# One layer of a hybrid decoder on one core: the two key blocks of the sliding window joined by a maximum before the turn, the convolution mix in two parts, and the transposes of the next rows spread over VectorE's list

## Chip, core and metric

The kernel runs on one core of a Trainium2 chip, in float32. The time is that of the device, in microseconds, from three runs. Engines: TensorE (PE, with its weight loads PEld), VectorE (DVE), ScalarE (ACT), GpSimd (POOL) and SyncE (SP), which issues most transfers.

## The reference

One layer over 1024 tokens of width 1024. The mixer has two head groups side by side, a gated short convolution (512 channels) and a sliding-window attention (8 query heads, 2 key heads, head size 64, window 128, blocks of 128 queries against the block before and their own); then a mixture of 32 experts, four for each token.

```python
h    = rms_norm(x, norm_mix)
proj = h @ w_in + b_in                      # B_gate | C_gate | u | q | k | v
y_conv = b_gate * causal_short_conv(c_gate * u, conv_w)
# attention: keys are [block before | own block], 256 of them
rel = qi[:, None] + BLOCK - kj[None, :]     # distance of query qi to key slot kj
in_window = (rel >= 0) & (rel < WINDOW)
logits = where(mask, scores + bias, -inf)
m = maximum(max(logits), sink)
p = exp(logits - m)
out = (p / (sum(p) + exp(sink - m))) @ v
mix = concatenate([rms_norm(y_conv), rms_norm(y_attn)])
x = x + mix @ w_out + b_out
x = x + moe_ffn(rms_norm(x, norm_ffn))      # top 4 of 32 experts
```

Window and block are both 128. For a query q and a place s of 0 to 127, key s of the block before is in the window only if s > q, and key s of the own block only if s <= q. Of the two keys at one place exactly one is ever seen (none of the block before in the first block).

## The kernel before

The function mixer handles the 1024 tokens in eight blocks of 128 rows: trip 0 (first=True), a hardware loop over trips 1 to 6, and trip 7 (more=False). The function experts follows it. Each engine has its own list of instructions in program order, written by hand in one_block of that engine; engines meet through semaphores only (wait, then_inc; then_wait makes VectorE wait for its own instruction). An engine whose next instruction waits does nothing behind it.

A trip on TensorE: the convolution's projections for four groups of 128 channels (project_conv, into ps_c), the turn of q and k (L978, L980), the scores (L989, into ps_s: 8 heads x 256 keys), the rest of project_conv, then turn_p (L925: sixteen transposes of 128x128 of the probabilities, eight for each half of four heads, into ps_q, ps_kv and two banks of ps_s), attend (L936, values times pT, into ps_c), the convolution's output mix (L1008, eight matmuls into ps_s, columns 0 to 1023) with the sum of squares of the convolution between its halves (L943), the sum of squares of the attention (L943), the attention's output mix (L1017, into the other half of ps_s), and the projections of q and of k, v for the next block (L885, L889), routing (L904, L1038) among them.

VectorE adds the bias to the scores (add_bias, L694), takes the maximum over 256 keys for each head (L780 and L787), finds the top with the sink (find_top), and adds and divides after the exponentials (normalise: L709, L713, multiply L714 for the first four heads, while ScalarE scales the second four, L574). gate_input (L664) and gate_output (L683) are the convolution's gates; groups 0 and 1 have their taps on VectorE, groups 2 and 3 on GpSimd (add_taps_pool, L456 to L462), which also scales the result into conv_s for the mix (L480 for groups 0 to 2, L484 for group 3). ScalarE takes the exponential (exp_half, L537). The turned probabilities are copied into pT: j=0 by VectorE (read_turned, L730), j=1 by ScalarE (turn_read_act, L544). VectorE turns the normed rows of the next block, xn, into hT by sixteen 32x256 transposes (turn_xn, L622), in parts of 4, 6 and 6; ScalarE scales them (L515), and project_q of the next trip waits for that (hT_ready). VectorE sums conv_sq (L801), makes attnT (L804), sums attn_sq (L809), then updates x1 twice (L824 after the convolution mix, L829 after the attention mix) and makes h2 (L834). GpSimd computes every power of -0.5 (L446) and, in trip 0, copies the bias of the block before over a mask (L474).

## Time and profile before

| | |
|---|---|
| three runs | 1985.57, 1989.87, 1989.88 us (median 1989.87) |
| profiled execution | 1985.67 us, span 1983.9 us |
| TensorE's mean granted clock | 0.988 of full |
| busy: TensorE, VectorE, ScalarE, GpSimd | 1921.2, 1294.7, 430.9, 238.2 us |
| mixer | the first 472 us or so of the span, eight trips |
| TensorE waits in trips 1 to 7 | 2.7 us in six waits of L936 for VectorE's pT, in the window 96 to 430 us |

A row of a timeline names the line of the code, the operation, the tiles out<-in, the size, how many instructions of a kind are merged, and in brackets how long the engine sat idle before it and what ended that. TensorE's instructions overlap: a group's end is modelled, and the start of the next group is the better mark. An f32 matmul shows as two instructions, a transpose as one. A row of busy times by stretch gives the stretch and its length, then busy time (and instructions) of PE, PEld, DVE, ACT and POOL, then the granted clock (1.00 is full), the busy share of the DMA engines, and GB/s.

### The profile page before, as it was taken

How to read it: one execution, taken by the hardware profiler on the slowest of the kernel's cores; microseconds unless marked ns; L12 is line 12 of the kernel's file. 1: busy time of each engine (PE TensorE's matmuls, PEld its weight loads, DVE VectorE, ACT ScalarE, POOL GpSimd, SP SyncE). 2: the span in 40 equal slices, each digit the busy share in tenths (PEclk: the TensorE clock that was granted, in tenths of full speed). 3: DMA queues.
4: the chain of work that ended last, by engine and by line, in shares of the span. 5: the costliest groups of instructions: out<-in, count | busy, mean ns of one | idle time of the engine just before them, and what ended most of it. 6: DMA issues, size and time to landing. Idle time of an engine off the chain costs nothing.

```text
span 1983.9 us, 33393 instructions
## 1 busy us (share of the span) xinstructions
PE 1921.2 (97%) x12288; PEld 1399.4 (71%) x12288; DVE 1294.7 (65%) x3725; ACT 430.9 (22%) x926; POOL 238.2 (12%) x317
## 2 busy tenths in 40 slices
PE   7999999998999999999999999999899999999996
PEld 5667777774999999999999999933334444444442
DVE  2777777774277777776666666644537766777665
ACT  1233333331121222222222222222312100001100
POOL 1212222211000111111111111110000000000000
PEclk8999999998999999999999999999999999999998
DMA  9411001002957787778888898899999999999992
GB/s 311 110 43 42 18 35 42 32 33 86 363 184 237 251 272 250 254 263 288 282 291 297 294 305 298 309 370 383 364 364 384 377 362 354 370 368 369 361 360 72
DMA packets 207682, 498.39 MB, mean 251 GB/s; under 512 B 7716, under 2 KB 14928, under 8 KB 200080
## 3 DMA queue, kind: packets, MB, share of 16 engines
q1 hardware_dynamic: 194016, 449.43, 62.9%
q0 software_dynamic: 11312, 39.85, 8.0%
q10 hardware_dynamic: 2304, 8.39, 1.0%
q8 instruction: 38, 0.62, 0.1%
q14 instruction: 12, 0.10, 0.0%
HBM read 470.24 MB, written 27.41 MB: 251 GB/s over the span
## 4 chain that ended last, share of the span: by engine, by line
issue 36%; PE 36%; POOL 1%; DMA 1%; DVE 1%; POOLq 0%; ACT 0%; DVEq 0%; ACTq 0%
PE ps_unit L1871 36%; POOL x_got L1363 1%; DMA x_got<-h_rows,idx_next 0%; DMA out_dram<-y_rows,idx_cur 0%; PE ps_list L1843 0%; POOL carrier L1359 0%; POOL out_dram L1420 0%; POOLq L1081 0%; POOL out_dram L1375 0%; DVE match L1547 0%; DVE reached L1595 0%; POOLq L1411 0%; POOLq L1250 0%; POOLq L1275 0%; DVE xT L1669 0%
## 5 line engine op out<-in xcount | busy, mean ns | idle before, releaser
L1871 PE MATMUL ps_unit<-xT,w_slot 128*128 128x136 f32 (+6 forms) x3840 | 521.4, 298 | 2.7 <-issue 2.7
L1871 PEld LDWEIGHTS ps_unit<-xT,w_slot 128*128 128x128 f32 x3840 | 516.7, 196 | 2.9 <-issue 2.9
L1901 PE MATMUL ps_unit<-w_slot,xT 128*128 128x512 f32 x704 | 306.7, 594 | 1.1 <-DVE xT L1264 1.1
L1264 DVE STREAM_TRANSPOSE xT<-x_got 32x256 f32<-32x256 f32 x644 | 280.5, 436 | 29.5 <-DMA x_got<-h_rows,idx_next 21.1
L1871 PE MATMUL ps_unit<-act_T,w_slot 128*128 128x136 f32 (+6 forms) x1920 | 261.6, 298 | 0.1
L1871 PEld LDWEIGHTS ps_unit<-act_T,w_slot 128*128 128x128 f32 x1920 | 257.9, 190 | 2.2 <-DVE act_T L1644 1.5
L1901 PEld LDWEIGHTS ps_unit<-w_slot,xT 128*128 128x128 f32 x704 | 132.8, 190 | 164.2 <-issue 164.2
L1660 DVE STREAM_TRANSPOSE y_rows<-yT 32x256 f32<-32x256 f32 x372 | 162.1, 436 | 55.0 <-ACT yT L1466 50.1
L914 PE MATMUL ps_c<-hT,w_in_sb 128*128 128x128 f32 x1536 | 182.5, 279 | 5.4 <-DMA w_in_sb<-in_w_in_dram 5.4
L914 PEld LDWEIGHTS ps_c<-hT,w_in_sb 128*128 128x128 f32 x1536 | 177.7, 194 | 10.7 <-DMA w_in_sb<-in_w_in_dram 6.3
L1359 POOL TENSOR_TENSOR carrier<-carrier 128x1 f32<-128x1 f32 x64 | 15.8, 247 | 1319.8 <-issue 610.6
L1914 PE MATMUL ps_unit<-w_slot,act_T 128*128 128x512 f32 x352 | 154.7, 592 | 0.0
L2031 PE MATMUL ps_unit<-w_slot,xT 128*32 128x512 f32 x1152 | 132.7, 619 | 13.9 <-DVE xT L1264 13.9
L1264 DVE STREAM_TRANSPOSE act_T<-act_rows 32x64 f32<-32x64 f32 x528 | 124.6, 236 | 7.9
L1634 DVE TENSOR_SCALAR glu<-ps_unit,b_cur 128x160 f32<-128x160 f32 (+1 forms) x120 | 50.4, 420 | 109.5 <-PE ps_unit L1871 109.0
L1914 PEld LDWEIGHTS ps_unit<-w_slot,act_T 128*128 128x128 f32 x352 | 66.0, 190 | 78.9 <-issue 78.9
L2031 PEld LDWEIGHTS ps_unit<-w_slot,xT 128*32 128x32 f32 x1152 | 37.9, 113 | 100.5 <-issue 100.3
L1459 ACT ACTIVATE sig<-glu 128x256 f32<-128x256 f32 x120 | 50.0, 417 | 241.9 <-DVE glu L1634 241.7
L1477 ACT ACTIVATE sig<-glu 128x256 f32<-128x256 f32 x44 | 18.3, 416 | 360.4 <-DVE glu L1724 360.4
L1466 ACT ACTIVATE yT<-ps_unit,b_cur 128x256 f32<-128x256 f32 x120 | 50.4, 471 | 208.4 <-PE ps_unit L1871 208.4
L1642 DVE TENSOR_TENSOR sig<-sig,glu 128x160 f32<-128x160 f32 (+1 forms) x120 | 43.7, 364 | 76.9 <-ACT sig L1459 73.5
L1787 DVE TENSOR_TENSOR hid<-ps_unit,b_row 128x512 f32<-128x512 f32 x18 | 12.3, 686 | 90.5 <-PE ps_unit L2031 90.5
(296 smaller groups left out, 1865.0 us busy)
## 6 DMA issues: line engine op xcount, KB each, us to landing
w_slot<-in_w_dram SPq DMA_DIRECT2D x192, 2048.0 KB, 11.1
b_row<-in_b_dram SPq DMA_DIRECT2D x11, 1024.0 KB, 12.9
w_in_sb<-in_w_in_dram SPq DMA_DIRECT2D x6, 1024.0 KB, 12.0
b_row<-in_b_dram SPq DMA_DIRECT2D x11, 512.0 KB, 15.2
x_in<-in_x_dram SPq DMA_DIRECT2D x8, 512.0 KB, 3.5
x_res<-in_x_dram SPq DMA_DIRECT2D x8, 512.0 KB, 4.7
out_dram<-x ACTq DMA_DIRECT2D x8, 512.0 KB, 5.0
h_rows<-h ACTq DMA_DIRECT2D x8, 512.0 KB, 3.1
```

The source lines that it names most:

```text
L914: last = pe.matmul(ps_c[:, c % 2, j * P:(j + 1) * P], w_in_sb[:, k, first:first + P], hT[:, k, :], start=(k == 0), stop=(k == KD - 1))
L1264: last = nc.vector.transpose(out[c * Q:(c + 1) * Q, :, tokens], rows.rearrange("p (k c j) -> p k c j", c=P // Q, j=Q)[:, :, c, :])
L1363: nc.gpsimd.indirect_dma_start(out=x_got[0:n, i, :], out_offset=None, in_=h2_rows, in_offset=bass.IndirectOffsetOnAxis(ap=idx_next[0:n, i: ...
L1459: nc.scalar.activation(sig[:, p % 3, :], glu[:, p % 3, :], ACT.Sigmoid, scale=ALPHA).then_inc(sig_ready[p].sem, 1)
L1466: last = nc.scalar.activation(yT[:, m, :], ps_unit[p % RING][:, u, :], ACT.Identity, bias=b2_cur[:, m:m + 1])
L1634: v.tensor_scalar(glu[:, p % 3, 0:n], ps_unit[p % RING][:, 0, 0:n], b1_cur[:, 2 * p:2 * p + 1], LIMIT, ALU.add, ALU.min).then_inc(glu_read ...
L1642: v.tensor_tensor(sig[:, p % 3, 0:n], sig[:, p % 3, 0:n], glu[:, p % 3, 0:n], ALU.mult).then_inc(scaled[p].sem, 1)
L1660: last = v.transpose(rows[:, :, c, :], yT[c * Q:(c + 1) * Q, :, a * Q:(a + 1) * Q])
L1871: last = pe.matmul(ps_unit[p % RING][:, u, 0:n], w, moving[:, k, 0:n], start=(k == 0), stop=(k == KD - 1))
L1901: last = pe.matmul(ps_hid[c], xT[:, k, 0:P], w_slot[:, c, k, :], start=(k == 0), stop=(k == KD - 1))
L1914: last = pe.matmul(ps_out[m], act_T[:, k, 0:P], w_slot[:, W1_LOADS + m, k, :], start=(k == 0), stop=(k == KD - 1))
L2031: last = pe.matmul(ps_flat[t][g * TILE:(g + 1) * TILE, :], xT[:, k, t * TILE:(t + 1) * TILE], w, start=(k == 0), stop=(k == KD - 1), tile_ ...
```

## The change

Attention: after the bias VectorE joins the two key blocks of each head, place by place, by a maximum into the first 128 columns of probs (join_keys), and reduces these 128 for the top. Exponentials, division and turn then run on 128 columns a head. turn_p has four transposes for each half, into ps_q and one bank of ps_s. VectorE reads each turned half twice, each time multiplied by a 0/1 mask keys_in (own block: tri + identity; block before: one minus that), so that pT has both key blocks again for attend. ScalarE's copies of pT are gone. keys_in is made once, in front of the loop.

TensorE: of the convolution's mix, channel groups 0 and 1 (both output halves) stand before attend, and groups 2 and 3 behind it; the sum of squares of the convolution follows the whole mix. The wait for conv_scaled is in front of the first part, that for conv_scaled_last in front of the second.

VectorE: the transposes of the next rows stand in parts of 2 (before the reads of the turned probabilities), 4, 6 and 4 (behind the mean of the squares, ahead of the first x1 update), where they were in parts of 4, 6 and 6 (the last behind the first x1 update).

```diff
--- before.py
+++ after.py
@@ -218,6 +218,7 @@
         conv_s = sb("conv_s", [P, CC, P])
         probs = sb("probs", [P, NH, 2 * P])
         pT = sb("pT", [P, 2, 2, HALF * P])
+        keys_in = sb("keys_in", [P, 2, P])
         attn_ss = sb("attn_ss", [P, P])
         attnT = sb("attnT", [P, CC, P])
         x1 = sb("x1", [P, D])
@@ -260,7 +261,7 @@
         ps_heads = ps_s[:].rearrange("p (h k) -> p h k", h=NH)
         ps_route = ps_s[:, 1024:1024 + NE]
         ps_parts = ps_s[:, 1536:1536 + P]
-        ps_turned = [[ps_q[:], ps_kv[:]], [ps_s[:, 1024:1536], ps_s[:, 1536:2048]]]
+        ps_turned = [ps_q[:], ps_s[:, 1024:1536]]
 
 
         early_loaded = sem("early_loaded")
@@ -316,7 +317,9 @@
         exped = [event(f"exped_{i}") for i in ("first", "second")]
         denom_ready = event("denom_ready_second")
         probs_ready = [event(f"probs_ready_{i}") for i in ("first", "second")]
-        p_turned = [[event(f"p_turned_{i}{j}") for j in range(2)] for i in ("first", "second")]
+        p_turned = [event(f"p_turned_{i}") for i in ("first", "second")]
+        joined = [event(f"keys_joined_{i}") for i in ("first", "second")]
+        keys_made = sem("keys_made")
         pT_ready = [[event(f"pT_ready_{i}{j}") for j in range(2)] for i in ("first", "second")]
         av_done = event("av_done")
         attn_squared = event("attn_squared")
@@ -534,14 +537,10 @@
                 wait(act, neg_ready[i], t)
                 for h in range(HALF):
                     s = HALF * i + h
-                    nc.scalar.activation(probs[:, s, :], probs[:, s, :], ACT.Exp, bias=neg_top[:, s:s + 1],
+                    nc.scalar.activation(probs[:, s, 0:P], probs[:, s, 0:P], ACT.Exp, bias=neg_top[:, s:s + 1],
                                          accum_out=row_sum[:, s:s + 1])
                 part = slice(i * HALF, (i + 1) * HALF)
                 nc.scalar.activation(sink_exp[:, part], sink_gap[:, part], ACT.Exp).then_inc(exped[i].sem, 1)
-
-            def turn_read_act(t, i):
-                wait(act, p_turned[i][1], t)
-                nc.scalar.copy(pT[:, i, 1, :], ps_turned[i][1]).then_inc(pT_ready[i][1].sem, 1)
 
             square_x(0)
             norm_x(0)
@@ -571,11 +570,9 @@
                 exp_half(t, 1)
                 wait(act, denom_ready, t)
                 for s in range(HALF, NH):
-                    last = nc.scalar.activation(probs[:, s, :], probs[:, s, :], ACT.Copy, scale=rdenom[:, s:s + 1])
+                    last = nc.scalar.activation(probs[:, s, 0:P], probs[:, s, 0:P], ACT.Copy, scale=rdenom[:, s:s + 1])
                 last.then_inc(probs_ready[1].sem, 1)
                 add_u_bias(t, 3)
-                turn_read_act(t, 0)
-                turn_read_act(t, 1)
                 wait(act, conv_out[3], t)
                 nc.scalar.activation(conv_sq[:], conv_y[:], ACT.Square).then_inc(conv_squared.sem, 1)
                 wait(act, attnT_ready, t)
@@ -694,6 +691,15 @@
                 nc.vector.tensor_tensor(probs[:, part, :], ps_heads[:, part, :], bias_all[:, part, :],
                                         ALU.add).then_inc(biased[i].sem, 1)
 
+            def join_keys(t, i):
+
+                part = slice(i * HALF, (i + 1) * HALF)
+                wait(dve, biased[i], t)
+                nc.vector.tensor_tensor(probs[:, part, 0:P], probs[:, part, 0:P], probs[:, part, P:2 * P],
+                                        ALU.max).then_inc(joined[i].sem, 1)
+                wait(dve, joined[i], t)
+                then_wait(t, nc.vector.tensor_reduce(denom[:, part], probs[:, part, 0:P], AX_X, ALU.max))
+
             def find_top(t, i):
 
                 part = slice(i * HALF, (i + 1) * HALF)
@@ -711,8 +717,8 @@
                     nc.vector.reciprocal(rdenom[:, part], denom[:, part]).then_inc(denom_ready.sem, 1)
                     return
                 then_wait(t, nc.vector.reciprocal(rdenom[:, part], denom[:, part]))
-                nc.vector.tensor_tensor(probs[:, part, :], probs[:, part, :],
-                                        rdenom[:, part].unsqueeze(2).broadcast_to([P, HALF, 2 * P]),
+                nc.vector.tensor_tensor(probs[:, part, 0:P], probs[:, part, 0:P],
+                                        rdenom[:, part].unsqueeze(2).broadcast_to([P, HALF, P]),
                                         ALU.mult).then_inc(probs_ready[i].sem, 1)
 
             def turn_h2(t):
@@ -725,9 +731,13 @@
                         last = nc.vector.transpose(h2T[c * 32:(c + 1) * 32, :, a * 32:(a + 1) * 32], rows[:, :, c, :])
                 last.then_inc(h2_squared_off.sem, 1)
 
-            def read_turned(t, i, j):
-                wait(dve, p_turned[i][j], t)
-                nc.vector.tensor_copy(pT[:, i, j, :], ps_turned[i][j]).then_inc(pT_ready[i][j].sem, 1)
+            def read_turned(t, i):
+                wait(dve, p_turned[i], t)
+                for j in range(2):
+                    nc.vector.tensor_tensor(pT[:, i, j, :].rearrange("p (h q) -> p h q", h=HALF),
+                                            ps_turned[i].rearrange("p (h q) -> p h q", h=HALF),
+                                            keys_in[:, j, :].unsqueeze(1).broadcast_to([P, HALF, P]),
+                                            ALU.mult).then_inc(pT_ready[i][j].sem, 1)
 
             dve.wait_ge(cleared, 6)
             x_to_mean(0)
@@ -752,6 +762,10 @@
             nc.vector.tensor_copy(bias_all[:, :, P:2 * P], ps_heads[:, :, P:2 * P]).then_inc(bias_flipped, 1)
             dve.wait_ge(bias_flipped, 2)
             nc.vector.tensor_copy(tri_b[:], cst[:, C_TRI:C_TRI + P])
+            nc.vector.tensor_tensor(keys_in[:, 1, :], cst[:, C_TRI:C_TRI + P], ident, ALU.add).then_inc(keys_made, 1)
+            dve.wait_ge(keys_made, 1)
+            nc.vector.tensor_scalar(keys_in[:, 0, :], keys_in[:, 1, :], -1.0, 1.0, ALU.mult, ALU.add).then_inc(keys_made, 1)
+            dve.wait_ge(keys_made, 2)
             nc.vector.tensor_copy(ones_b[:], cst[:, C_ONES:C_ONES + P])
             nc.vector.scalar_tensor_tensor(out=token[:], in0=cst[:, C_TOK:C_TOK + NB], scalar=32.0,
                                            in1=cst[:, C_TOK + NB:C_TOK + 2 * NB], op0=ALU.mult, op1=ALU.add)
@@ -776,27 +790,27 @@
                 if not first:
                     dve.wait_ge(bias_switched, 1)
                 add_bias(t, 0)
-                wait(dve, biased[0], t)
-                then_wait(t, nc.vector.tensor_reduce(denom[:, 0:HALF], probs[:, 0:HALF, :], AX_X, ALU.max))
+                join_keys(t, 0)
                 wait(dve, scored[1], t)
                 add_bias(t, 1)
                 find_top(t, 0)
                 add_taps(t, 1)
                 gate_output(t, 1)
-                wait(dve, biased[1], t)
-                then_wait(t, nc.vector.tensor_reduce(denom[:, HALF:NH], probs[:, HALF:NH, :], AX_X, ALU.max))
+                join_keys(t, 1)
                 find_top(t, 1)
                 normalise(t, 0)
                 gate_input(t, 2)
                 normalise(t, 1)
                 gate_output(t, 2)
                 gate_input(t, 3)
-                read_turned(t, 0, 0)
-                read_turned(t, 1, 0)
+                if more:
+                    wait(dve, x_normed, t + 1)
+                    turn_xn(t + 1, 0, 2)
+                read_turned(t, 0)
+                read_turned(t, 1)
                 gate_output(t, 3)
                 if more:
-                    wait(dve, x_normed, t + 1)
-                    turn_xn(t + 1, 0, 4)
+                    turn_xn(t + 1, 2, 4)
                 wait(dve, conv_squared, t)
                 nc.vector.tensor_reduce(conv_ss[:], conv_sq[:].rearrange("p c q -> p q c"), AX_X,
                                         ALU.add).then_inc(conv_joined.sem, 1)
@@ -809,11 +823,13 @@
                 nc.vector.tensor_reduce(attn_ss[:], attn_sq.rearrange("p c q -> p q c"), AX_X,
                                         ALU.add).then_inc(attn_joined.sem, 1)
                 if more:
-                    turn_xn(t + 1, 4, 6)
+                    turn_xn(t + 1, 6, 6)
                 wait(dve, attn_summed, t)
                 wait(dve, conv_summed, t)
                 then_wait(t, nc.vector.tensor_copy(ss_ca, ps_kv[:, 2 * P:2 * P + 2]))
                 mean(ss_ca, ms_ca, CW).then_inc(ca_mean.sem, 1)
+                if more:
+                    turn_xn(t + 1, 12, 4)
                 wait(dve, conv_mixed, t)
                 wait(dve, ca_rstd, t)
                 wait(dve, res_biased, t)
@@ -823,8 +839,6 @@
                 dve.wait_ge(late_loaded, all_late)
                 then_wait(t, nc.vector.scalar_tensor_tensor(out=x1[:], in0=ps_s[:, 0:D], scalar=rstd_ca[:, 0:1],
                                                             in1=x_res[:], op0=ALU.mult, op1=ALU.add))
-                if more:
-                    turn_xn(t + 1, 10, 6)
                 wait(dve, attn_mixed, t)
                 nc.vector.scalar_tensor_tensor(out=x1[:], in0=ps_s[:, D:2 * D], scalar=rstd_ca[:, 1:2],
                                                in1=x1[:], op0=ALU.mult, op1=ALU.add).then_inc(x1_ready.sem, 1)
@@ -919,11 +933,17 @@
             def turn_p(t, i):
 
                 wait(pe, probs_ready[i], t)
-                for j in range(2):
-                    for h in range(HALF):
-                        s = HALF * i + h
-                        last = pe.transpose(ps_turned[i][j][:, h * P:(h + 1) * P], probs[:, s, j * P:(j + 1) * P], ident)
-                    last.then_inc(p_turned[i][j].sem, 1)
+                for h in range(HALF):
+                    last = pe.transpose(ps_turned[i][:, h * P:(h + 1) * P], probs[:, HALF * i + h, 0:P], ident)
+                last.then_inc(p_turned[i].sem, 1)
+
+            def mix_conv(ks):
+
+                for n in range(2):
+                    for k in ks:
+                        last = pe.matmul(ps_s[:, n * 512:(n + 1) * 512], conv_s[:, k, :],
+                                         w_out_sb[:, k, n * 512:(n + 1) * 512], start=(k == 0), stop=(k == CC - 1))
+                return last
 
             def attend(t):
 
@@ -997,19 +1017,14 @@
                 project_conv(t, 3)
                 for i in range(2):
                     turn_p(t, i)
-                attend(t)
                 wait(pe, conv_scaled, t)
                 wait(pe, biased[1], t)
                 pe.wait_ge(out_w_loaded, 48)
-                for n in range(2):
-                    for k in range(CC):
-                        if n == 0 and k == CC - 1:
-                            wait(pe, conv_scaled_last, t)
-                        last = pe.matmul(ps_s[:, n * 512:(n + 1) * 512], conv_s[:, k, :],
-                                         w_out_sb[:, k, n * 512:(n + 1) * 512], start=(k == 0), stop=(k == CC - 1))
-                    if n == 0:
-                        sum_squares(t, conv_joined, conv_ss, 0, conv_summed)
-                last.then_inc(conv_mixed.sem, 1)
+                mix_conv((0, 1))
+                attend(t)
+                wait(pe, conv_scaled_last, t)
+                mix_conv((2, 3)).then_inc(conv_mixed.sem, 1)
+                sum_squares(t, conv_joined, conv_ss, 0, conv_summed)
                 sum_squares(t, attn_joined, attn_ss, 1, attn_summed)
                 wait(pe, attnT_ready, t)
                 for n in range(2):
```

## Rows read from the trace of the kernel before

**Rows 1.** The page, busy time of each engine: us (share of the span) xinstructions.
```profile
PE 1921.2 (97%) x12288; PEld 1399.4 (71%) x12288; DVE 1294.7 (65%) x3725; ACT 430.9 (22%) x926; POOL 238.2 (12%) x317
```

**Rows 2.** Busy time by stretch, trip 4: us; PE, PEld, DVE, ACT, POOL; clock, DMA.
```profile
266.00:320.00 54.00, 53.55 (x324) 38.96 (x324) 40.27 (x97) 18.34 (x50) 11.37 (x17) 1.00 0.11 39
```

**Rows 3.** Timeline of TensorE, trips 0 and 4: start us, duration us, what [idle before].
```profile
63.67 1.94 PE L936 MATMUL ps_c<-pT,v_keys 128*64 128x512 f32 x8 [0.46 <-DVE pT L730]
...
80.96 3.24 PE L885 MATMUL ps_q<-w_in_sb,hT 128*128 128x512 f32 x7 [0.67 <-ACT hT L515]
...
279.21 0.60 PE L925 MATMUL ps_q<-cst,probs 128*128 128x128 f32 x4
...
280.08 1.04 PE L925 MATMUL ps_s<-cst,probs 128*128 128x128 f32 x8
...
281.57 1.94 PE L936 MATMUL ps_c<-pT,v_keys 128*64 128x512 f32 x8 [0.45 <-DVE pT L730]
...
283.44 3.70 PE L1008 MATMUL ps_s<-w_out_sb,conv_s 128*128 128x512 f32 x8
...
290.63 0.28 PE L943 MATMUL ps_kv<-cst,attn_ss 128*128 128x1 f32 x2
...
290.77 7.11 PE L1017 MATMUL ps_s<-w_out_sb,attnT 128*128 128x512 f32 x16
...
297.82 7.10 PE L885 MATMUL ps_q<-w_in_sb,hT 128*128 128x512 f32 x16
```

**Rows 4.** Timeline of VectorE, trip 4.
```profile
260.64 0.69 DVE L651 TENSOR_TENSOR qn<-qk,small 128x512 f32<-128x512 f32 x1 [2.08 <-POOL small L446]
...
268.90 1.22 DVE L780 TENSOR_REDUCE small<-probs 128x4 f32<-128x1024 f32 x1
...
274.59 0.16 DVE L709 TENSOR_TENSOR small<-small 128x4 f32<-128x4 f32 x1
...
275.00 1.22 DVE L714 TENSOR_TENSOR probs<-probs,small 128x1024 f32<-128x1024 f32 x1
...
276.14 0.34 DVE L664 SCALAR_TENSOR_TENSOR conv_x<-ps_c,vectors,conv_u 128x128 f32<-128x128 f32 x1
...
276.92 0.41 DVE L709 TENSOR_TENSOR small<-small 128x4 f32<-128x4 f32 x1 [0.44 <-ACT small L540]
...
278.78 0.35 DVE L683 SCALAR_TENSOR_TENSOR conv_y<-ps_c,vectors,conv_t 128x128 f32<-128x128 f32 x1 [1.23 <-POOL conv_t L462]
...
279.88 0.35 DVE L664 SCALAR_TENSOR_TENSOR conv_x<-ps_c,vectors,conv_u 128x128 f32<-128x128 f32 x1 [0.74 <-ACT conv_u L529]
...
280.74 0.68 DVE L730 COPY pT<-ps_s 128x512 f32<-128x512 f32 x1
...
284.58 1.05 DVE L801 TENSOR_REDUCE conv_ss<-conv_sq 128x128 f32<-128x512 f32 x1
...
285.55 0.68 DVE L804 TENSOR_TENSOR attnT<-ps_c,vectors 128x512 f32<-128x512 f32 x1
...
286.89 1.03 DVE L809 TENSOR_REDUCE attn_ss<-qk_sq 128x128 f32<-128x512 f32 x1 [0.66 <-ACT qk_sq L582]
...
293.67 2.70 DVE L622 STREAM_TRANSPOSE hT<-xn 32x256 f32<-32x256 f32 x6
```

**Rows 5.** Timeline of ScalarE, trip 4.
```profile
277.58 1.70 ACT L574 ACTIVATE probs<-probs,small 128x256 f32<-128x256 f32 x4 [0.69 <-DVE small L711]
...
296.40 2.44 ACT L515 ACTIVATE hT<-hT,vectors 128x128 f32<-128x128 f32 x8 [9.54 <-DVE hT L622]
```

**Rows 6.** Timeline of GpSimd, trips 0 and 4.
```profile
63.12 0.83 POOL L480 TENSOR_TENSOR conv_s<-conv_y,vectors 128x384 f32<-128x384 f32 x1
...
276.56 1.11 POOL L456 TENSOR_TENSOR conv_t<-conv_x,vectors 128x128 f32<-128x128 f32 x3 [8.90 <-DVE conv_x L664]
...
279.36 0.83 POOL L480 TENSOR_TENSOR conv_s<-conv_y,vectors 128x384 f32<-128x384 f32 x1 [0.62 <-DVE conv_y L683]
```

**Rows 7.** Busy time by stretch, at the start of the expert stage.
```profile
485.00:490.00 5.00, 4.23 (x21) 2.17 (x22) 3.09 (x17) 0.54 (x2) 2.00 (x2) 0.50 0.27 79
```

## The prediction

> **What bounds the kernel now.** The page comes first: TensorE is busy for 97% of the span [rows 1]. That says little about a single stage, because the change lies in the mixer alone, which is the first 470 us or so. Next comes the table by stretches, cut to one trip of the token block loop. From trip 0 to trip 4 the projection of q moves from 80.96 to 297.82, so a trip takes 54.2 us [rows 3]. Of 54.0 us in trip 4 TensorE is busy 53.5, VectorE 40, ScalarE 18 and GpSimd 11, at a granted clock of 1.00 [rows 2]. So a trip ends when TensorE's own list ends, and the change is worth what it takes off that list, less the waits that it puts in. The timeline of TensorE over the attention's end is read third, for starts rather than busy time, since the ends of matmuls are modelled [rows 3]. The other three engines are read last, each for when it delivers what TensorE will ask for [rows 4 to 6].
>
> **The path that is shortened.** From the first turn of probabilities at 279.21 to the attention's output mix at 290.77 TensorE takes 11.56 us. Its terms are sixteen transposes (279.21 to 280.08 is eight, 0.87, so 1.74 in all, to 280.95), a gap until 281.57 (0.62, ended by the copies of pT; the view shows 0.45 of it as idle), attend (281.57 to 283.44, 1.87), and from there 7.33 for two sums of squares of 0.14 each (290.63 to 290.77) and eight matmuls of the convolution mix, so 3.53 for four of them [rows 3].
>
> **Eight transposes fewer.** They save 0.87 us of that path in each trip. Nothing lies beside them that would keep the time: what they waited for, probs_ready of the second half, is set by ScalarE's four scalings, which end at 279.28 [rows 5]. The turn of the second half would now start at 279.64, and with 128 columns in place of 256 the scalings and exponentials end sooner, not later.
>
> **The gap of 0.62 us.** It is there because attend follows the turn at once and VectorE has to bring the turned blocks over first. In the new order half of the convolution mix (four matmuls, 3.53 us) stands between, and that covers the copies, if it can start. What is late next is conv_s, the input of this half: GpSimd writes it.
>
> **When conv_s comes.** TensorE is through with eight transposes at 279.21 + 0.87 = 280.08. Before, conv_s was done at 279.36 + 0.83 = 280.19, and nobody asked for it before 283.44 [rows 3, 6]. It hangs on a chain: VectorE's gate_input(2) at 276.14, GpSimd's taps from 276.56, gate_output(2) at 278.78, GpSimd at 279.36 [rows 4, 6]. Before gate_input(2) VectorE changes as follows. Each half had a maximum over 128x1024 (268.90, 1.22 us, next start after 1.26). It gets a join over 128x512 and a reduction over 128x512. The trace has no such operations; the nearest are a tensor_tensor of 128x512 from SBUF with 0.69 [rows 4] and, for the reduction, the halved streaming part of the 1.22, about 0.68. With 0.03 for the wait behind each, a half takes 1.43 in place of 1.26: +0.17, twice +0.34. The multiply of the first half's probabilities falls from 1.22 (start to start 1.14) to 0.69 (0.61): -0.53. Net -0.19, so gate_input(2) is at 275.95 and conv_s is done at 280.00. TensorE behind a semaphore started 0.15 after the producer's end (copy 280.74 + 0.68 = 281.42, attend at 281.57), so the mix starts near 280.2: a new wait g of about 0.1 us. There are two more waits in front of this matmul, which may cost a little each; I take g = 0.15. Its bounds: nothing (0.0), if the chain is 0.1 faster; and above, if the reduction costs as much as the strided one of 128x512 (1.05 instead of 0.68, twice [rows 4]), g = 0.15 + 0.74 = 0.9.
>
> **The copies of pT.** ScalarE's two copies go; VectorE has four tensor_tensor with a PSUM source instead of two copies of 0.68 (start to start 0.60, as the multiply's 1.22 gave 1.14). A PSUM source with a broadcast operand is shown by attnT: 0.68 [rows 4]. VectorE: gate_input(3) at 279.88, two transposes 0.89 from 280.14, four reads 2.40 from 281.03 to 283.43, the last result at 283.51. The mix half ends at 280.23 + 3.53 = 283.76, so attend finds all four. Attend runs to 285.63, the second mix half to 289.16, and its last input (conv_s of channel 3) comes from gate_output(3) at 283.43, ended 283.78, plus 0.23 and at most the 0.83 of three groups on GpSimd [rows 6]: 284.8, in time.
>
> **The spread transposes.** Behind gate_output(3) VectorE has four (1.78) to 285.47, the sum over conv_sq (0.97) to 286.44, attnT to 287.12, 0.66 for ScalarE's square to 287.78, the sum over attn_sq (1.03) to 288.81. TensorE asks for it at 289.16 + 0.14 = 289.30. This is 0.35 us of room after latency, where there were 2.7 before (done at 287.92, asked for at 290.63 [rows 3, 4]): the second place to watch. Then six transposes (2.67) to 291.5, the mean (0.3), four more (1.78) to 293.6. hT is complete at 293.6 and no longer at 293.67 + 2.70 = 296.37 [rows 4]. TensorE will want the scaled hT at 289.44 + 7.05 = 296.5 and ScalarE needs half of 2.44 us for its first half [rows 5], so this is free. It must be: before, ScalarE scaled from 296.40, so that hT_ready came at 297.6 and project_q started at 297.82, and a TensorE that is 1.3 us earlier would have run into it. The moved transposes are what lets the gain through.
>
> **Behind the mix.** The second x1 update, h2, its transposes, routing and q/k norms all follow attn_mixed on one chain, which shifts as a whole. The mask keys_in is built once, two VectorE operations of 128 columns in a stretch where VectorE waits for the first convolution weights at the start: nothing, an estimate from their size alone.
>
> **Sum.** A trip: 0.87 + 0.62 - 0.15 = 1.34 us less (bounds 0.6 to 1.5). Trips 1 to 6 and the last one, whose attention is built the same: 7 x 1.34 = 9.4. Trip 0 differs: GpSimd also switches the bias there, so conv_s is done at 63.12 + 0.83 = 63.95 [rows 6], and attend had started at 63.67 [rows 3]. The new order waits until about 63.93 (conv_s 0.19 earlier, plus latency); then 3.53 + 1.87 + 3.53 + 0.28 lead to 73.14 and 7.05 more to 80.19, where project_q had started at 80.96, with 0.67 idle for hT before it. That is 0.8 less. Together 10.2 us. The profiled execution took 1985.67 (span 1983.9), so 1975.5 on its scale. The three timed runs are 1985.57, 1989.87 and 1989.88: the profiled one stands with the lowest, and the median is 4.2 higher. By the median the sum gives 1979.7, by the profile 1975.5; I say **1978**.
>
> **A rule weighed.** An add of 128x4 of two SBUF operands took 0.16 us at 274.59 and 0.41 at 276.92, when GpSimd's taps ran beside it [rows 4, 6]. The Trainium skill, page "SBUF — State Buffer", section on the two separate sides, says that VectorE with two SBUF inputs and a GpSimd instruction that reads SBUF exclude each other for a whole instruction. By that rule, with which the two adds agree, a join could be held or hold the taps. The joins fall at about 268.9 and 273.2, when GpSimd is idle (its taps start at 276.56 [rows 6]), so by rule and row alike the sum stays as it is; were one join per trip held by one tap operation of 0.4 us, the gain would be about 7 us, which is inside rival 1.
>
> **Rivals.** (1) *The wait moves to GpSimd.* The join and reduction cost more than taken, g is 0.5 to 1.0, and a trip gives 0.5 to 1.0 us: seven of them 3.5 to 7, with trip 0's 0.8 some 6 less in all, 1984 by the median. For it: conv_s has no room at all now. Against: every price of 512 columns from SBUF is near 0.7, except the strided reduction. Chance 0.2. (2) *Slower.* The join and the reduction over every second 128 columns run at the price of the 1024-column ones, 1.22 each. Then gate_input(2) is 4 x 0.53 = 2.1 us later, g is 2.25, and a trip loses 2.25 - 1.49 = 0.76: 8 x 0.76 = 6 us more, 1996. It decides from g = 1.49 on. Against it: the ordinary operations are priced by what they stream. Chance 0.05. (3) *The gain is lost behind the mixer.* At the start of the expert stage the clock is granted at half, 0.50 of full from 485 to 490 us [rows 7]; the stage starts earlier against whatever decides on the clock, and the first unit could see the low level for some microseconds more; five at half rate lose 2.5 of work, and as much again if the weights' units behind it slip; I take 5. The three runs, 4.3 apart, show that something of this size is drawn anew. Then 1983 to 1985. Chance 0.13. (4) *The masked read does not fit the room* before the sum over attn_sq: with 0.2 more for each of the four reads, TensorE waits 0.45 a trip, which leaves 0.9 and about 7 us, 1983. Chance 0.07.
>
> **From this the numbers.** Forecast (9 to 12 us less, all mechanisms as told): 0.55. The range is 1971 to 1986: below, the full gain with no new wait on the lower scale (1974) and 3 us of draw; above, rivals 1, 3 and 4. A measurement of this kernel can tell about 0.3%, 6 us, from no change. Faster by more: the forecast, half of the rivals 1 and 4, a third of rival 3: 0.73. Within: the rest of these, 0.21. Slower: rival 2 and a hundredth of rival 3: 0.06.
>
> **What will show it.** TensorE's turn has eight transposes and is followed by mix matmuls within 0.3 us; the stretch to the attention mix is near 10.2 us; a trip is near 52.9 us. Its largest releaser in the loop is GpSimd's conv_s and not VectorE's pT; VectorE's last transpose of hT ends 3 us before project_q. The join and the short reduction are each near 0.69. Wrong if TensorE sits over 0.5 us before the mix or before the sum of squares, if project_q waits for hT, or if the expert stage, from its first weights to its end, is longer than before.

## The result

The changed kernel takes 1975.72 us (median of four runs, 1975.15 to 1976.06); the kernel before, four runs by then, 1988.82 (1985.57 to 1989.88). The ratio is 0.9936, with a 95% interval of 0.9923 to 0.9948: faster by 0.64%. The forecast was 1978, from 1971 to 1986. The profiled execution took 1975.62 us with a span of 1973.8, 10.1 less than before; the sum in the prediction said 10.2. (How much of that agreement is luck is said further down.)

TensorE's timeline of the changed kernel in trip 4, from the turn of the probabilities to the next projection (start, duration, what; compare [rows 3]):

```profile
273.92 0.60 PE L937 MATMUL ps_q<-cst,probs 128*128 128x128 f32 x4
...
274.80 3.70 PE L944 MATMUL ps_s<-w_out_sb,conv_s 128*128 128x512 f32 x8
...
278.43 1.94 PE L956 MATMUL ps_c<-pT,v_keys 128*64 128x512 f32 x8
...
280.30 3.70 PE L944 MATMUL ps_s<-w_out_sb,conv_s 128*128 128x512 f32 x8
...
283.98 0.36 PE L963 MATMUL ps_kv<-cst,attn_ss 128*128 128x1 f32 x2
...
284.20 7.11 PE L1032 MATMUL ps_s<-w_out_sb,attnT 128*128 128x512 f32 x16
...
291.15 7.03 PE L899 MATMUL ps_q<-w_in_sb,hT 128*128 128x512 f32 x16
```

Eight transposes, then at once four matmuls of the mix, with no idle time shown before any of these groups. From the turn (273.92) to the attention mix (284.20) it is 10.28 us, where it was 11.56. From there to project_q it is 6.95, where it was 7.05. The first project_q of the loop, with the wait of trip 0 in front of its mix:

```profile
63.60 3.70 PE L944 MATMUL ps_s<-w_out_sb,conv_s 128*128 128x512 f32 x8 [1.50 <-POOL conv_s L483]
...
79.95 4.46 PE L899 MATMUL ps_q<-w_in_sb,hT 128*128 128x512 f32 x10
```

project_q moves from 79.95 in trip 0 to 291.15 in trip 4, so a trip takes 52.80 us instead of 54.21. VectorE, GpSimd and ScalarE in the same trip (compare [rows 4 to 6]):

```profile
263.61 0.69 DVE L698 TENSOR_TENSOR probs<-probs 128x512 f32<-128x512 f32 x1
...
264.33 0.69 DVE L701 TENSOR_REDUCE small<-probs 128x4 f32<-128x512 f32 x1
...
273.34 0.35 DVE L680 SCALAR_TENSOR_TENSOR conv_y<-ps_c,vectors,conv_t 128x128 f32<-128x128 f32 x1 [1.23 <-POOL conv_t L465]
...
275.74 1.29 DVE L737 TENSOR_TENSOR pT<-ps_q,keys_in 128x512 f32<-128x512 f32 x2
...
276.94 1.28 DVE L737 TENSOR_TENSOR pT<-ps_s,keys_in 128x512 f32<-128x512 f32 x2
...
286.78 1.79 DVE L619 STREAM_TRANSPOSE hT<-xn 32x256 f32<-32x256 f32 x4
```
```profile
273.92 0.83 POOL L483 TENSOR_TENSOR conv_s<-conv_y,vectors 128x384 f32<-128x384 f32 x1 [0.62 <-DVE conv_y L680]
```
```profile
288.61 2.45 ACT L518 ACTIVATE hT<-hT,vectors 128x128 f32<-128x128 f32 x8 [6.03 <-DVE hT L619]
```

conv_s is done at 273.92 + 0.83 = 274.75 and TensorE uses it at 274.80. The masked reads lie at 275.74 to 278.2, beside the first mix part. The last transposes of the next rows end at 288.57, ScalarE's first half of hT 1.2 later, and TensorE asks at 291.15, so hT now has 1.3 us of room.

The mixer ends (first instruction of the expert stage on TensorE) at 461.98, where it was 472.77: 10.8 less. The expert stage takes 1511.8 us from there instead of 1511.1.

### The profile page after: what moved, and what is told of

Read it like the earlier page. It is cut to its first block, busy times and chain, and to the rows that moved or that the text cites. A ratio compares the mean times of both kernels' runs of the same rounds, so it can differ in the third digit from the quotient of the medians.

```text
span 1973.8 us, 33290 instructions
## 1 busy us (share of the span) xinstructions
PE 1912.5 (97%) x12224; PEld 1390.5 (70%) x12224; DVE 1302.9 (66%) x3759; ACT 411.4 (21%) x910; POOL 238.3 (12%) x317
## 4 chain that ended last, share of the span: by engine, by line
PE 39%; issue 35%; POOL 1%; DVE 1%; DMA 0%; POOLq 0%; ACT 0%; DVEq 0%; ACTq 0%
PE ps_unit L1886 38%; POOL x_got L1378 1%; DMA x_got<-h_rows,idx_next 0%; PE ps_list L1858 0%; POOL carrier L1374 0%; POOL out_dram L1435 0%; POOLq L1096 0%; DVE match L1562 0%; POOL out_dram L1390 0%; DVE reached L1610 0%; POOLq L1426 0%; POOLq L1265 0%; DVE xT L1684 0%; ACT xT L1466 0%; POOLq L1413 0%
```

## The experiments

Each was profiled and timed beside the kernel before on the same chip, and the ratios given are to those runs. The changed kernel was not timed again beside them, so its median and theirs come from different sets of runs. Three figures are read for each: the median; the trip, which is the distance of project_q in trips 0 and 6 divided by six; and the mixer's end. The trip is the sharpest. The median also holds the length of the expert stage, which no experiment touches and which lay between 1509.9 and 1516.5 us in the fourteen profiles, with no relation to what had been done in the mixer. The mixer's end also holds what comes ahead of the turn of trip 0, where TensorE waits for the first transfers: that turn started anywhere from 60.21 to 61.98 us (61.30 before, 61.06 in the changed kernel). Where it matters, the end is therefore also counted from that turn.

### Three parts, alone and in pairs

The change has three parts that can stand alone: the join (128 columns, four transposes a half, masked reads), the split mix, and the spread transposes.

**The changed kernel without the spread.** In place of parts of 2, 4, 6, 4:

```diff
-    turn_xn(t + 1, 0, 2)          # ahead of read_turned
-    turn_xn(t + 1, 2, 4)          # behind gate_output(t, 3)
+    turn_xn(t + 1, 0, 4)
-    turn_xn(t + 1, 6, 6)          # behind the sum over attn_sq
+    turn_xn(t + 1, 4, 6)
-    turn_xn(t + 1, 12, 4)         # behind the mean
+    turn_xn(t + 1, 10, 6)         # behind the first x1 update
```

> The changed kernel with the next rows' transposes back in parts of 4, 6 and 6, the last part behind the first x1 update; join and split mix stay. Theory (the gain of TensorE's shorter list passes only because hT is done earlier): VectorE would finish the sum over attn_sq near 282.8 on the clock of the changed kernel's trip 4, six transposes to 285.5, the first x1 update to 288.0 (it waits for GpSimd's root), six transposes to 290.7; ScalarE's first half of the scaling takes 1.2 more, to 292.0, and TensorE asks at 291.15. So project_q waits 0.9 us in each of seven trips: 6 us more than the changed kernel, about 1982, the page names ScalarE's hT as releaser. Rival (hT had room, the new parts are decoration): no wait, 1975.7.

Measured: 1983.9 us, ratio to before 0.9974 (0.9964 to 0.9984), a trip of 54.08. The page of waits names ScalarE's hT six times in six trips, and the timelines of TensorE and VectorE show the chain as it was expected, 0.2 us longer:

```profile
289.00 7.11 PE L1030 MATMUL ps_s<-w_out_sb,attnT 128*128 128x512 f32 x16
...
297.19 7.11 PE L897 MATMUL ps_q<-w_in_sb,hT 128*128 128x512 f32 x16 [1.09 <-ACT hT L518]
```
```profile
291.73 1.28 DVE L836 SCALAR_TENSOR_TENSOR x<-ps_s,small,x_res 128x1024 f32<-128x1024 f32 x1 [1.04 <-POOL small L449]
...
293.05 2.69 DVE L619 STREAM_TRANSPOSE hT<-xn 32x256 f32<-32x256 f32 x6
```

project_q starts 8.19 us after the attention mix and not 6.95. Of the 1.41 us a trip that the whole change brings, 1.28 hang on the moved transposes (54.08 less 52.80). The rival, that hT had room, falls.

**The changed kernel without the split.**

```diff
-    wait(pe, conv_scaled, t)      # and biased, out_w_loaded
-    mix_conv((0, 1))
     attend(t)
-    wait(pe, conv_scaled_last, t)
-    mix_conv((2, 3)).then_inc(conv_mixed.sem, 1)
+    wait(pe, conv_scaled, t)
+    # the eight matmuls as before, sum_squares between the halves
```

> The changed kernel with the convolution mix whole and behind attend, as before; join and spread transposes stay. Theory (the split covers VectorE's four masked reads, which alone hold the second half's first block until 277.6, while the turn ends at 274.8): attend waits 2.8 us a trip and the stretch from turn to attention mix is 12.9 instead of 10.28, trips 1 to 6 lose 2.65 each, the last 1.8 (no transposes of next rows in front of the reads), trip 0 1.0 (conv_s no longer waited for): 19 more, about 1994, slower than the kernel before. Rival (the split only covers the 0.6 us of wait that was there before): 0.5 us a trip, 4 in all, 1980.

Measured: 2000.96 us, ratio 1.0056 (1.0039 to 1.0073). The wait is the expected one, 2.82 us in every trip. But the median is 25 us above that of the changed kernel and not 19, and in the profiled run, the slowest of the four, the mixer ends 28.2 later. The timeline of TensorE shows two kinds of trips; here trips 3 and 4:

```profile
234.42 1.94 PE L956 MATMUL ps_c<-pT,v_keys 128*64 128x512 f32 x8 [2.82 <-DVE pT L737]
...
236.29 3.70 PE L1028 MATMUL ps_s<-w_out_sb,conv_s 128*128 128x512 f32 x8
...
290.00 2.70 PE L956 MATMUL ps_c<-pT,v_keys 128*64 128x512 f32 x8 [2.82 <-DVE pT L737]
...
292.63 4.59 PE L1028 MATMUL ps_s<-w_out_sb,conv_s 128*128 128x512 f32 x8
```

In trip 3 attend takes its usual 1.94 and the mix half 3.70; in trip 4 they take 2.70 and 4.59, behind the same idle 2.82 us. The busy times by stretch of trip 4 have the granted clock in the third number from the end:

```profile
288.00:290.00 2.00, 0.01 (x1) 0.04 (x1) 2.00 (x4) 0.00 (x0) 1.27 (x3) 1.00 0.00 0
...
290.00:292.00 2.00, 2.00 (x8) 0.53 (x8) 1.94 (x5) 0.63 (x1) 1.22 (x2) 0.76 0.00 0
...
292.00:294.00 2.00, 2.00 (x4) 0.84 (x3) 1.97 (x4) 0.00 (x0) 1.49 (x1) 0.50 0.00 0
...
296.00:298.00 2.00, 2.00 (x7) 0.98 (x6) 1.95 (x5) 0.00 (x0) 0.00 (x0) 1.00 0.00 0
```

Behind the gap the granted clock falls to 0.50, the lower of its two levels (1.2 instead of 2.4 GHz), and it is back at 1.00 by 296. project_q follows project_q after 55.57 us in one trip (195.00 to 250.57) and after 57.23 in the next (250.57 to 307.80); this alternates through all trips. So the wait costs 2.77 a trip by itself, and 1.66 more in every second trip through the clock. Why only every second trip, no run shows. The gap of 0.45 in the kernel before, of 1.92 in the next experiment and of 1.35 with the spread alone left the clock at 1.00 in all six trips of the loop. In front of each of these gaps TensorE ran transposes only: from the first of them to attend it is 3.86 us here, 2.96 in the join alone and 3.26 in the spread alone. No run tells which of the two, the idle time or the whole stretch, goes with the fall.

**The join alone** (both edits above together).

> The kernel before with the join alone (128 columns, four transposes a half, masked reads by VectorE); mix whole, transposes of the next rows in parts of 4, 6, 6. Theory (the removed transposes turn into a longer wait for the masked reads): the reads' third result comes near 276.8 with a turn that ends at 274.8, so attend waits 2.0 us where it waited 0.6; a trip loses 0.5 of that net of the 0.87 saved and wins 0.1 at hT: 3 us more than the kernel before in all, about 1988 to 1991. Rival (eight transposes fewer are worth their 0.87 wherever they stand): 7 us less than before, 1979.

```profile
280.20 0.60 PE L935 MATMUL ps_q<-cst,probs 128*128 128x128 f32 x4
...
283.16 1.94 PE L954 MATMUL ps_c<-pT,v_keys 128*64 128x512 f32 x8 [1.92 <-DVE pT L737]
...
285.03 3.70 PE L1026 MATMUL ps_s<-w_out_sb,conv_s 128*128 128x512 f32 x8
...
299.41 7.10 PE L897 MATMUL ps_q<-w_in_sb,hT 128*128 128x512 f32 x16
```

Measured: 1990.23 us, ratio 1.0011 (1.0001 to 1.0022), a trip of 54.81, 0.60 more than before. The turn is 0.87 us shorter and the wait behind it 1.92 long instead of 0.45. The join by itself is a small loss, and the rival of 7 us saved is out by far.

**The split alone** (the split's edit made in the kernel before).

> The kernel before with the mix split in two and nothing else. Theory (hT is the next limit): the 0.6 us of wait for pT goes, but attend ends 3 us later, attnT and the sum over attn_sq with it (to 288.8 instead of 287.9 on the clock of trip 4), and with them the last transposes (to 296.7) and hT's first half (298.0, where TensorE would ask at 297.2 and started at 297.8 before). A trip wins nothing or loses 0.2: 0 to 1.5 more than before. The page names ScalarE's hT as releaser in every trip. Rival (the wait for pT was the loss): 0.5 a trip less, 4 us less than before.

```profile
282.46 3.60 PE L932 MATMUL ps_s<-w_out_sb,conv_s 128*128 128x512 f32 x8
...
291.75 7.11 PE L1020 MATMUL ps_s<-w_out_sb,attnT 128*128 128x512 f32 x16
...
299.95 7.10 PE L885 MATMUL ps_q<-w_in_sb,hT 128*128 128x512 f32 x16 [1.09 <-ACT hT L515]
```

Measured: 1990.86 us, ratio 1.0012 (1.0003 to 1.0022), a trip of 54.84. The direction is the expected one, the size is not: 0.63 a trip and not 0 to 0.2. The stretch to the attention mix is 0.52 shorter, but from there to project_q it is 8.20, 1.15 longer. The expectation had put hT's first half at 298.0 on the clock of the kernel before. The trace, 1.5 later as a whole, has it at 298.53 + 1.25 = 299.8 at the earliest and project_q at 299.95, thus 0.45 later than expected. Two thirds of that lie on VectorE, whose last transposes end at 298.49, which is 297.0 on the old clock where 296.7 had been counted; the rest is the 0.15 from ScalarE's first half to project_q.

**Split and spread without the join.**

> The kernel before with split mix and spread transposes, without the join: sixteen transposes a trip, 256 columns. Theory (the two orders together free the 0.6 us of wait for pT and the hidden 0.1 to 0.2 at hT, the join adds only the eight transposes' 0.87): 0.7 us a trip, 5.5 in all, about 1980 by the profiled scale. Rival (the join is what makes the orders pay): no gain, 1985 to 1988.

Measured: 1983.18 us, ratio 0.9976 (0.9965 to 0.9987), a trip of 53.56 (0.65 less), the mixer's end 466.56 (6.2 less). TensorE has no wait in the loop. Counted from the turn of trip 0, 1.09 us earlier here than before, the mixer is 5.1 shorter, and the medians are 4.2 apart (1987.39 for the kernel before beside it). The profiled run was the slowest of the eight (1984.86), with the longest expert stage of all, 1516.5.

**The spread alone.**

> The kernel before with the next rows' transposes spread and nothing else: the missing corner of the table of three parts. Theory (a spread that puts two transposes ahead of the copies of pT, with no mix half to cover them, lengthens the wait for pT by their 0.89, against 0.17 won at hT): a trip 54.9 instead of 54.2, the mixer's end 4.5 later than before, about 1990, releaser VectorE's pT with 1.3 us. Rival (more room for hT is a gain by itself): 0.17 a trip less, trip 0 0.8, 2 less than before.

```profile
284.84 1.94 PE L938 MATMUL ps_c<-pT,v_keys 128*64 128x512 f32 x8 [1.35 <-DVE pT L730]
...
300.99 7.03 PE L887 MATMUL ps_q<-w_in_sb,hT 128*128 128x512 f32 x16
```

Measured: 1992.02 us, ratio 1.0021 (1.0011 to 1.0031), a trip of 54.99, the mixer's end 4.65 later. This is as expected: project_q comes 6.95 after the attention mix (0.1 won) and attend waits 1.35 instead of 0.45.

The eight corners together:

| join | split | spread | trip, us | mixer's end, us | to before | to before, from trip 0's turn |
|---|---|---|---|---|---|---|
| | | | 54.21 | 472.77 | | |
| x | | | 54.81 | 476.17 | +3.4 | +4.1 |
| | x | | 54.84 | 475.65 | +2.9 | +3.7 |
| | | x | 54.99 | 477.42 | +4.7 | +4.4 |
| x | x | | 54.08 | 470.60 | -2.2 | -1.8 |
| x | | x | 56.40 | 490.20 | +17.4 | +18.2 |
| | x | x | 53.56 | 466.56 | -6.2 | -5.1 |
| x | x | x | 52.80 | 461.98 | -10.8 | -10.6 |

Each part alone makes the mixer slower. The three together make it faster by more than any pair does.

### The terms, one by one

**Eight transposes put back** in the changed kernel:

```diff
     last.then_inc(p_turned[i].sem, 1)
+    spare = [ps_kv[:], ps_s[:, 1536:2048]][i]
+    for h in range(HALF):
+        pe.transpose(spare[:, h * P:(h + 1) * P], probs[:, HALF * i + h, P:2 * P], ident)
```

> The changed kernel with the eight dropped transposes put back, of the unused second 128 columns into free banks that nobody reads: the price of eight transposes by itself. Theory: 0.87 a trip less what conv_s was late by (0.1 at most), so 0.8; in trip 0 the wait for conv_s of 1.5 hides them: 7 x 0.8 = 5.6 more, 1981.3. Rival (the transposes lie beside a wait that would be there anyway): less than 2 us more.

```profile
275.94 0.60 PE L937 MATMUL ps_q<-cst,probs 128*128 128x128 f32 x4
...
277.68 3.60 PE L947 MATMUL ps_s<-w_out_sb,conv_s 128*128 128x512 f32 x8
...
281.21 1.94 PE L959 MATMUL ps_c<-pT,v_keys 128*64 128x512 f32 x8
```

Measured: 1982.9 us (0.9981, 0.9971 to 0.9991), a trip of 53.56, 0.76 more than the changed kernel. The turn takes 0.87 more (275.94 to 277.68 is 1.74), and the first mix part 0.10 less (3.53 instead of 3.63), because conv_s is then there long before. That is 0.77. The mixer's end moves by 5.0, or 5.3 from trip 0's turn. A trip of 53.56 is also what split and spread have without the join: all that the join wins is these transposes, and its other halvings (exponentials, maxima, scalings) win nothing on TensorE's list.

**conv_s later by one GpSimd instruction:**

```diff
     wait(pool, conv_mixed, t - 1)
+    nc.gpsimd.tensor_tensor(scratch[:], conv_y[:, 0:3, :], conv_g_col...)   # 128x384, then wait
     nc.gpsimd.tensor_tensor(conv_s[:, 0:3, :], ...)
```

> The changed kernel with one more GpSimd instruction of 128x384 (0.83 us, result unused) in front of the one that makes conv_s: the wait for conv_s lengthened by a known piece. Theory (conv_s has no room: it is ready as the turn ends): the whole of 0.87 shows in each of eight trips, 7 us more, 1982.7, releaser GpSimd's conv_s. Rival (conv_s comes well ahead and its closeness in the trace is chance): under 2 us more.

```profile
277.51 0.60 PE L942 MATMUL ps_s<-cst,probs 128*128 128x128 f32 x4
...
278.87 3.70 PE L949 MATMUL ps_s<-w_out_sb,conv_s 128*128 128x512 f32 x8 [0.75 <-POOL conv_s L488]
```

Measured: 1981.64 us (0.9968, 0.9956 to 0.9979), a trip of 53.70, so the whole delay shows (0.90 a trip, for 0.87 put in). The mixer's end is 6.8 later, or 7.2 from trip 0's turn. conv_s has no room.

**The sum over attn_sq done twice:**

```diff
     wait(dve, attn_squared, t)
+    nc.vector.tensor_reduce(scratch[:], attn_sq..., AX_X, ALU.add)          # then wait
     nc.vector.tensor_reduce(attn_ss[:], attn_sq..., AX_X, ALU.add)
```

> The changed kernel with the sum over attn_sq done twice (first into a scratch tile), 1.07 us more on VectorE in front of attn_joined. Theory (the room there is 0.3 us in trips 1 to 6, 1.2 in trip 0, and several us in the last): TensorE waits 0.75 in six trips, 4.5 us more, 1980.2; hT still has room and takes nothing. Rival (VectorE's delay also reaches hT or the x1 chain): a whole 1.07 or more in each of seven trips, 7.5 us more.

```profile
287.61 0.38 PE L968 MATMUL ps_kv<-cst,attn_ss 128*128 128x1 f32 x2 [0.63 <-DVE attn_ss L828]
...
294.81 5.74 PE L904 MATMUL ps_q<-w_in_sb,hT 128*128 128x512 f32 x13
```

Measured: 1979.29 us (0.9953, 0.9936 to 0.9969), a trip of 53.61, 0.81 longer for 1.07 put in. So the room there was 0.26, and 0.3 had been counted. hT, which VectorE delivers behind it, did not get a wait (project_q again 6.95 behind the attention mix).

### Further edits to the changed kernel

**The switch of the bias in trip 0 behind conv_s** (GpSimd's L477 of the changed kernel moved two lines down).

> The changed kernel with GpSimd's switch of the bias in trip 0 behind conv_s of groups 0 to 2 instead of in front. Theory: trip 0's wait of 1.5 us for conv_s goes, and what is next there (the sum over attn_sq, ready at 71.6, asked for at 71.4) leaves 1.4: 1974.3. Rival (the microseconds of trip 0 are given back at the start of the expert stage, whose first transfers come when they come): 1975.7.

```profile
60.24 0.60 PE L937 MATMUL ps_q<-cst,probs 128*128 128x128 f32 x4
...
71.11 0.38 PE L963 MATMUL ps_kv<-cst,attn_ss 128*128 128x1 f32 x2 [0.49 <-DVE attn_ss L823]
...
78.30 1.88 PE L899 MATMUL ps_q<-w_in_sb,hT 128*128 128x512 f32 x4
```

Measured: 1973.76 us (0.9937, 0.9923 to 0.9951). From the turn to project_q trip 0 takes 18.06 us instead of 18.89: 0.83 won and not 1.4, because the sum over attn_sq is asked for earlier and now has a wait of 0.49 there. The timed runs are too coarse for it: the ratio to the kernel before is that of the changed kernel (0.9936), and the 2 us between the medians are from two sets of runs. In the profile the turn of trip 0 also starts earlier (60.24 for 61.06), within what it varies by without any edit.

**conv_s in two parts that match the two parts of the mix:**

```diff
+    for i in range(2):
+        wait(pool, conv_out[i], t)
+    wait(pool, conv_mixed, t - 1)
+    nc.gpsimd.tensor_tensor(conv_s[:, 0:2, :], ...).then_inc(conv_scaled.sem, 1)
     add_taps_pool(t, 2)
     ...
-    nc.gpsimd.tensor_tensor(conv_s[:, 0:3, :], ...).then_inc(conv_scaled.sem, 1)
     add_taps_pool(t, 3)
-    nc.gpsimd.tensor_tensor(conv_s[:, 3:4, :], ...).then_inc(conv_scaled_last.sem, 1)
+    nc.gpsimd.tensor_tensor(conv_s[:, 2:4, :], ...).then_inc(conv_scaled_last.sem, 1)
```

> The changed kernel with conv_s made in two parts that match the two parts of the mix: groups 0 and 1 in front of the taps of group 2 (their inputs are there 3 us earlier), groups 2 and 3 at the end. Theory: conv_s is off the path in every trip; trip 0 wins 1.4, the others the 0.09 by which the first mix half was longer than the second: 2.0 less, 1973.7. Against it: GpSimd's new instruction reads beside VectorE's join of the second half, and if one holds the other by 0.6 us, group 2's gate comes later; that has over 1 us of room now, since nothing of group 2 is asked for before the second mix half.

Measured: 1971.96 us in five runs (1971.12 to 1972.77), ratio to before 0.9926 (0.9912 to 0.994); the changed kernel's four runs lie at 1975.15 to 1976.06, but its ratio, 0.9936 (0.9923 to 0.9948), is not clear of this one. What shows the gain is the trace. A trip is 52.68, 0.12 less, and trip 0 takes 17.13 from the turn to project_q, 1.76 less. Together 2.6, where 2.0 was expected, and 2.6 is also what the mixer's end gains from trip 0's turn. The first mix part takes 3.53 again in every trip. GpSimd's two instructions of one shape, the first beside VectorE's join (266.02 to 266.70), the second not:

```profile
266.24 0.93 POOL L475 TENSOR_TENSOR conv_s<-conv_y,vectors 128x256 f32<-128x256 f32 x1 [5.76 <-issue]
...
276.69 0.61 POOL L488 TENSOR_TENSOR conv_s<-conv_y,vectors 128x256 f32<-128x256 f32 x1 [1.30 <-DVE conv_y L681]
```
```profile
266.02 0.68 DVE L699 TENSOR_TENSOR probs<-probs 128x512 f32<-128x512 f32 x1
```

The same 128x256 takes 0.93 and 0.61, and so it is in all eight trips (0.93 or 0.94 against 0.61). 0.93 less 0.61 is 0.32, and the join ends 0.46 after GpSimd's start. The Trainium skill, page "SBUF — State Buffer", section on the two separate sides, says that of a VectorE instruction with two SBUF inputs and a GpSimd instruction that reads SBUF the one that starts first holds the other off until it is through. The rows agree in kind: the join started first, and GpSimd was the slower for it. In size they don't quite: 0.61 from the join's end on would have ended 0.14 later than it did. No row shows why.

**The sum of squares of the convolution between the output halves,** on top of that (the sum behind the first of them and not behind both).

> As the kernel with early scaling, and the convolution's sum of squares between the two output halves of the second mix part instead of behind them, so that the two sums are not back to back (0.22 us for the second, where it was 0.14 alone). Theory: 0.08 a trip, 0.6 more saved, 1973.1. Rival: the 0.22 is a wait for attn_joined, and then nothing is saved.

```profile
278.98 1.98 PE L1029 MATMUL ps_s<-w_out_sb,conv_s 128*128 128x512 f32 x4
...
280.80 0.28 PE L964 MATMUL ps_kv<-cst,conv_ss 128*128 128x1 f32 x2
...
282.74 0.28 PE L964 MATMUL ps_kv<-cst,attn_ss 128*128 128x1 f32 x2
...
282.88 7.11 PE L1038 MATMUL ps_s<-w_out_sb,attnT 128*128 128x512 f32 x16
```

Measured: 1972.1 us (six runs, 1968.54 to 1974.55; 0.9924, 0.991 to 0.9938), a trip of 52.68, the same as without it. The second sum is back at 0.14, but from 278.98 to 282.88 it is 3.90, and it was 3.90 before (278.31 to 282.21). So the 0.22 was no wait for attn_joined. Moving the first sum between the halves wins nothing: what the second sum has less, the mix around the first has more. What the 0.08 is the price of stays open.

## Why the prediction was right

**The list of TensorE.** The prediction took 0.87 us off for the transposes, 0.62 for the gap, and put 0.15 in for conv_s: 1.34 a trip. Measured in the stretch: 1.28. The transposes are confirmed by putting them back (0.87 in the turn), the gap by its absence. The new wait is no wait in the view: conv_s comes at 274.75 and the matmul starts 0.05 later, not 0.15 (0.05 also in trip 0 and with conv_s delayed, where TensorE does wait), and what is left is a first mix part that is 0.10 longer (3.63 for 3.53; 3.53 again once conv_s comes early). What the prediction did not have is 0.08 more for the two sums, which stand side by side now; parting them did not win it back.

**hT.** The prediction let project_q start 7.05 behind the attention mix, as before, and its figures left hT 0.2 us of room there (ready at 297.6, used at 297.82). It had none: in every kernel with the spread project_q starts after 6.95, and the split alone lost 1.15 there. The mechanism ("a TensorE that is 1.3 us earlier would have run into it") is what the kernel without the spread shows. It is the step on which most of the gain hung: without it 8.6 of the 10.8 us of the mixer are gone. The 0.10 won at hT, and 0.04 ahead of the turn, stood in no term. They more than make up for the 0.06 by which the stretch fell short, and a trip came to 1.41 less, not 1.34.

**conv_s.** Predicted done at 280.00, with the turn ending at 280.08, on the clock of the kernel before; that is 0.08 ahead of the end. The trace has 274.75 against 273.92 + 0.87 = 274.79: 0.04 ahead. The prices of the unseen operations held: join 0.69, reduction 0.69 (0.68 taken), multiply 0.69. Rival 1 (the wait moves to GpSimd) has its place right, as the delay of 0.87 that came out whole shows, and not its size (0.10 a trip for its 0.5 to 1.0); rival 2 (slower, at the price of 1024 columns) falls with the 0.69.

**The second place.** Room before the sum over attn_sq: 0.35 predicted, 0.26 by the experiment. The reads cost 0.60 from start to start, as taken, so rival 4 falls.

**Trip 0.** Predicted: conv_s waited for until 63.93, project_q 0.8 earlier. Measured: a mix start of 63.60 behind a wait of 1.50, and project_q at 79.95, 1.0 earlier, of which 0.24 is the earlier start of the turn (61.06 for 61.30): 0.77.

**Behind the mixer.** Rival 3 (the gain is lost at the start of the expert stage) did not happen in the way it was told. The stage's low clock is there in both kernels, and it moved with the stage. The edges of the low stretch, before and in the changed kernel (the clock is the third number from the end; between the two edges it is 0.50 throughout):

```profile
480.00:481.00 1.00, 0.00 (x0) 0.00 (x0) 0.93 (x9) 0.00 (x0) 0.00 (x0) 0.66 0.00 0
...
490.00:491.00 1.00, 1.00 (x2) 0.30 (x2) 0.00 (x0) 0.00 (x0) 0.00 (x0) 0.72 1.04 408
```
```profile
469.00:470.00 1.00, 0.00 (x0) 0.00 (x0) 0.90 (x8) 0.00 (x0) 0.00 (x0) 0.66 0.00 0
...
479.00:480.00 1.00, 1.00 (x3) 0.51 (x2) 0.00 (x0) 0.00 (x0) 0.21 (x1) 0.72 1.01 393
```

The same fall and the same return, ten microseconds apart in both, and 11 us earlier in the changed kernel: it lost nothing by the clock there. The first unit of the experts started at 490.11 instead of 502.48, thus 1.6 us more was won than in the mixer, and 2.3 us were lost again behind it: the stage took 0.7 us more in all. The prediction had named that as a sign of being wrong (an expert stage that is longer than before, from its first weights to its end), and from the first unit on it is: 1483.7 for 1481.4. In the other twelve profiles, which leave the stage alone, that length lies between 1481.7 and 1487.0, and the kernel before has the shortest of all fourteen, so the 2.3 can't be laid to the change. What makes the stage vary is open.

**The other signs.** The stretch (10.28 for "near 10.2"), the trip (52.80 for "near 52.9"), the join and the short reduction (0.69) came as told. Two did not. In the loop of the changed kernel TensorE waits for nothing, so conv_s is not its largest releaser there; its 1.50 us stand in trip 0 only. And VectorE's last transposes end 2.6 us before project_q (288.57 for 291.15), not 3.

**The sum, and what of it is luck.** The sum was made on the profiled execution and came out there to 0.1 us (1975.5 for 1975.62). That it is 0.1 is luck. The mixer gave 10.8 and not 10.2 (10.6 from trip 0's turn, and 0.24 by an earlier start of that turn, which is chance), and the expert stage took 0.7 of it back, out of a spread of several microseconds. The choice of 1978, halfway to the median, was the part that missed by 2.3: the changed kernel's four runs lie within 0.9 us at the lower scale. What draws 1985.6 or 1989.9 in the kernel before is not settled. 24 of its runs, taken beside the first experiments, spread from 1982.4 to 1991.1, and the length of the expert stage varies by itself in the profiles; no run here was made to tell why.

**Not tried:** dropping the masks or the exponentials' second half without the join; nothing in the table above needs it.

## What to carry to other kernels

Where one engine's list is the bound, a removed piece is only worth something if whoever feeds the next instruction is as early: find the producer that is late next for each place at which the bound engine arrives earlier, and price its room from the trace (here none at conv_s, 0.26 us at the sum, none at hT). Edits that each lose alone can win together, when each opens the room that another needs; judge them as a set, and take them out one at a time afterwards. And where work is split in two, split what feeds it in the same way: that was worth another 2.6 us of the mixer here, most of it (1.8) in trip 0.

## What was not expected of the hardware

A gap of 2.82 us on TensorE, behind eight transposes, was followed by a granted clock of 0.50 in every second trip only, at 1.66 us each; gaps of 1.92, 1.35 and 0.45 us never were. A GpSimd instruction of 128x256 took 0.93 us beside VectorE's two-input join and 0.61 without it. The two sums of squares, one moving column each, stood 0.14 us apart from the next group when large matmuls lay between them and took 0.36 for the pair side by side, yet the stretch around them was 3.90 us either way.
